# Compressed attention branch moved between the attention tiles, first token tile's heads finished ahead of the last tile

## The chip, the cores and the metric

The kernel runs on one core of one Trainium2 chip. The metric is device time in microseconds (us) for one execution. Five engines work side by side, each through its own queue in program order: TensorE (PE, matmuls and transposes), VectorE (DVE), ScalarE (ACT), GpSimd (POOL) and SyncE (SP, which issues the weight loads). They meet only through counting semaphores.

## The reference, cut to what matters

A decoder trunk of two layers, 256 tokens, model width 1024. Each layer is a mixer and a gated feed-forward network, each followed by a LayerNorm of `ALPHA*x + y`. The mixer's input projection feeds two halves. One is a short gated convolution of 512 channels. The other is attention of 8 query heads of 64 in 2 key/value groups with three branches:

```python
out = g0 * o_cmp + g1 * o_slc + g2 * o_win      # g = sigmoid(gates), per token and head
mixed = head_rmsnorm(concat([conv_out, attn_out]), head_norm_g)
x = layer_norm(ALPHA * x + mixed @ w_out)
```

`o_slc` and `o_win` are causal softmax attention over up to 256 keys. (At this length all blocks are selected and the window covers everything, so they differ only in their keys and values.) `o_cmp` is softmax attention over 15 compressed blocks of keys and values, which a small MLP makes out of 32 tokens each; a token sees only the blocks that have ended.

## The kernel before

**Tiles.** Tokens lie in two tiles `t` of 128. Projections are float32 products split in three (`mm3`: high by high, high by low, low by high). Weights come as 1 MB units through three `raw` buffers; ACT makes the high half of a unit (`split_hi`, L286), DVE the low half (`split_lo`, L290), into six ring slots.

**Attention units.** The two large branches are cut into 12 units `n` (`ATT`): branch, token tile, group, heads. Unit n goes through PE `scores` (banks 0 and 1 by parity) -> DVE `maxima` (L831, L833) -> ACT `exps` (L484) -> PE `transpose_p` (L1226, banks 6 and 7) -> DVE `copy_pT` (L841) -> PE `times_v` (L1239, into bank 2). `combine` on DVE (L849 to L863) weights what is summed in bank 2 and adds it to `acc`, once per branch and token tile (`og` 0 to 3, after units 1, 5, 7 and 11).

**Order.** The order on every engine is written out by hand. In PE's loop, step n issues `scores(n+2)`, `transpose_p(n+1)`, pieces of the convolution's projection, and `times_v(n)`. In DVE's loop, step n issues `maxima(n+1)`, `copy_pT(n)` and then what `between[n]` lists. In ACT's loop, step n issues `exps(n)` and then its own `between[n]`. Since queues are in order, what stands in `between[n]` of an engine is ahead of that engine's next unit.

**Compressed branch (thirteenth unit).** At PE's step 10, after `mean_squares(1)`, `cmp_scores` issues 24 matmuls of 30 columns into bank 0. After the loop DVE adds the mask, takes and subtracts the maximum (L1072 to L1078), ACT takes the exponential (L628), DVE sums, forms the factors and multiplies (L1082 to L1088). PE transposes (L1296), DVE copies, PE multiplies by the values (`times_v_cmp`, L1305, banks 7 and 2), DVE adds to `acc` (L881).

**Convolution and heads.** `mean_squares` (L1318), `copy_squares` (L895), POOL's `root` (L676, L678), `roots_high` and `roots_low`, `conv_roots` (L1328), `normalise_conv` (L906) and `mix_conv` / `mix_conv_low` (L498, L909) bring the convolution's heads to `xh`/`xl`. The attention heads of tile t go through ACT `square_heads` (L508), DVE `head_squares` (L886), POOL `root`, DVE `scale_heads` (L891), PE `heads_T` (L1348, bank 6+t), ACT `mix_high` and DVE `mix_low`. Both tiles' heads are done after the loop. Between these PE issues the output projection: `out_part(L, t, n, part)` is 6 matmuls of 512 columns on k-tile 2n+part, `out_unit` two of them. When tile 0's are all done (`y1_done`), DVE starts its LayerNorm while PE goes on with tile 1.

Of the kernel before, what the change touches and what calls it, by code (L numbers as in the profile page):

```python
# [59 lines left out]
N_ATT = 13  # L60
# [66 lines left out]
def build(nc, x, w_in, short_conv_w, cmp_pe, cmp_w1, cmp_b1, cmp_w2, cmp_b2, head_norm_g, w_out, ln1_g, ln1_b,  # L127
# [4 lines left out]
    with ExitStack() as ctx:  # L132
# [66 lines left out]
        smax = sb("smax", [P, N_ATT - 1, NPAIR])  # L199
# [24 lines left out]
        CMP_BANK = (7, 2)  # L224

# [25 lines left out]
        s_done, max_done, exp_done, cmp_p = sem("s_done"), sem("max_done"), sem("exp_done"), sem("cmp_p")  # L251
# [15 lines left out]


# [125 lines left out]
        def _(act):  # L394
# [109 lines left out]

            def square_heads(L, t):
# [48 lines left out]
            for L in range(DEPTH):  # L554
# [53 lines left out]
                for g in range(NG):  # L608
# [21 lines left out]
                mix_conv(L, 1)  # L630
                for t in range(TT):
                    square_heads(L, t)
                for t in range(TT):
                    act.wait_ge(mixT_done, 2 * L + t + 1)
                    for j in range(4):
                        mix_high(4 + j, xh[:, 4 + j, P * t:P * (t + 1)], bank[6 + t][:, P * j:P * (j + 1)])

                act.wait_ge(pv_done, 14 * L + 14)
# [27 lines left out]
        def _(pool):  # L666
# [57 lines left out]
        def _(dve):  # L724
# [110 lines left out]
            def copy_pT(L, n):  # L835
                dve.wait_ge(pT_done, N_ATT * L + n + 1)
                if n >= 2:
                    dve.wait_ge(pv_done, 14 * L + n - 1)
                width = 512 if n < 12 else 2 * P
                rows = P if n < 12 else NH * NBLK  # L840
                V.tensor_copy(probsT[n % 2][0:rows, 0:width], bank[6 + n % 2][0:rows, 0:width]).then_inc(pT_copied, 1)  # L841

            def combine(L, og, chain):
# [10 lines left out]
                dve.wait_ge(pv_done, 14 * L + O_READY[og])  # L854
# [5 lines left out]
                else:  # L860
                    V.tensor_tensor(part[:, 0, :].rearrange("p (h d) -> p h d", h=NH), o, c, ALU.mult).then_inc(o_read, 1)
                    dve.wait_ge(o_read, 4 * L + og + 1)
                    chain.mark(V.tensor_tensor(acc[:, t, :], acc[:, t, :], part[:, 0, :], ALU.add))  # L863
# [13 lines left out]
            def add_cmp(L, t, chain):  # L877

                dve.wait_ge(pv_done, 14 * L + 13 + t)
                chain.wait()  # L880
                V.tensor_tensor(acc[:, t, :], acc[:, t, :], bank[CMP_BANK[t]][:], ALU.add).then_inc(att_summed, 1)  # L881

# [28 lines left out]
            def mix_conv_low(L, pair):  # L911
                for j in (2 * pair, 2 * pair + 1):
                    dve.wait_ge(mix_hi, 12 * L + j + 1)
                    mix_low(j, xl[:, j, :], xh[:, j, :], conv_o[:, j, :])

# [68 lines left out]
            for L in range(DEPTH):  # L984
# [52 lines left out]
                for g in range(NG):  # L1037
# [13 lines left out]
                           3: [lambda: copy_squares(L, 0), lambda: split_lo(V, L, 15)], 4: [lambda: conv_gate(L, 1)],  # L1051
                           5: [lambda: split_lo(V, L, 16)],
                           6: [lambda: combine(L, 1, chain), lambda: split_lo(V, L, 17)],
                           7: [lambda: roots_low(L, 0), lambda: conv_taps(L, 1, chain)],
                           8: [lambda: combine(L, 2, chain), lambda: normalise_conv(L, 0)],
                           9: [lambda: conv_product(L, 1), lambda: mix_conv_low(L, 0)], 10: [lambda: split_lo(V, L, 18)]}
# [6 lines left out]
                copy_squares(L, 1)  # L1063
                split_lo(V, L, 19)
                copy_pT(L, 11)
                dve.wait_ge(s_done, N_ATT * L + 13)
                dve.wait_ge(pT_done, N_ATT * L + 11)
                flat = probs[0][:, 0:TT * NH * NBLK].rearrange("p (h c) -> p h c", c=NBLK)
                sc = probs[0][:, 0:TT * NH * NBLK].rearrange("p (t h c) -> p t h c", t=TT, h=NH)
                scores = bank[0][:, 0:TT * NH * NBLK].rearrange("p (t h c) -> p t h c", t=TT, h=NH)  # L1070
                for t in range(TT):
                    ins = V.tensor_tensor(sc[:, t], scores[:, t], bcast(cst[:, C_MA + NBLK * t:C_MA + NBLK * (t + 1)], 1,  # L1072
                                                                        [P, NH, NBLK]), ALU.add)
                chain.mark(ins)
                chain.wait()
                chain.mark(V.tensor_reduce(cmax[:], flat, AX.X, ALU.max))
                chain.wait()
                V.tensor_tensor(flat, flat, bcast(cmax[:], 2, [P, TT * NH, NBLK]), ALU.subtract).then_inc(max_done, 1)  # L1078
                roots_low(L, 1)
                dve.wait_ge(exp_done, N_ATT * L + 13)  # L1080
                for t in range(TT):
                    ins = V.tensor_reduce(rsum[:, 2, t].rearrange("p (g i) -> p i g", g=NG),  # L1082
                                          sc[:, t].rearrange("p (i g) c -> p i g c", g=NG), AX.X, ALU.add)
                chain.mark(ins)
                chain.wait()
                factors_cmp(L, chain)
                for t in range(TT):
                    ins = V.tensor_tensor(sc[:, t].rearrange("p (i g) c -> p i g c", g=NG),  # L1088
                                          sc[:, t].rearrange("p (i g) c -> p i g c", g=NG),
                                          coef[:, 2, t].rearrange("p (g i) -> p i g", g=NG).unsqueeze(3)  # L1090
                                          .to_broadcast([P, NPAIR, NG, NBLK]), ALU.mult)
                ins.then_inc(cmp_p, 1)
                combine(L, 3, chain)
                copy_pT(L, 12)
                normalise_conv(L, 1)
                for t in range(TT):
                    add_cmp(L, t, chain)
                head_squares(L, 0)
                mix_conv_low(L, 1)
                head_squares(L, 1)  # L1100
                for t in range(TT):
                    scale_heads(L, t)
                for t in range(TT):
                    dve.wait_ge(mix_hi, 12 * L + 8 + 4 * t)
                    for j in range(4):
                        tok = slice(P * t, P * (t + 1))
                        mix_low(4 + j, xl[:, 4 + j, tok], xh[:, 4 + j, tok], bank[6 + t][:, P * j:P * (j + 1)])
# [43 lines left out]
        def _(pe):  # L1151
# [128 lines left out]
            def cmp_scores(L):  # L1280

                pe.wait_ge(exp_done, N_ATT * L + 11)
                pe.wait_ge(cmp_copied, 2 * L + 1)
                for t in range(TT):
                    for h in range(NPAIR):
                        c0 = NG * NBLK * (NPAIR * t + h)
                        tok = slice(P * t, P * (t + 1))
                        ins = mm3(bank[0][:, c0:c0 + NG * NBLK], qTh[:, h, tok], qTl[:, h, tok],
                                  *(a[:].rearrange("p g c -> p (g c)") for a in (kcTh, kcTl)), True, True)
                ins.then_inc(s_done, 1)  # L1290

            def transpose_cmp(L):
                pe.wait_ge(cmp_p, L + 1)
                pe.wait_ge(pT_copied, N_ATT * L + 11)
                for t in range(TT):
                    ins = pe.transpose(bank[6][0:NH * NBLK, P * t:P * (t + 1)],  # L1296
                                       probs[0][:, NH * NBLK * t:NH * NBLK * (t + 1)], ident)
                ins.then_inc(pT_done, 1)

            def times_v_cmp(L, t):  # L1300
                pe.wait_ge(pT_copied, N_ATT * L + 13)
                pe.wait_ge(cmp_copied, 2 * L + 2)
                if t:
                    pe.wait_ge(o_read, 4 * L + 4)
                pe.matmul(bank[CMP_BANK[t]][:], probsT[0][0:NH * NBLK, P * t:P * (t + 1)], vbd.rearrange("p h d -> p (h d)"),  # L1305
                          start=True, stop=True).then_inc(pv_done, 1)
# [15 lines left out]
            def conv_roots(L, pair):  # L1322

                pe.wait_ge(roots_lo, 2 * L + pair + 1)
                for m in range(2):
# [6 lines left out]
            def out_product(L, t, c, k):  # L1332

                wh, wl = w_view(L, U_OUT + k // 2, 2)
# [323 lines left out]
```

## Time and profile before

| | |
|---|---|
| Median of 3 runs | 713.83 us (712.39 to 713.88) |
| Profiled execution, its own time | 709.42 us |
| Its span, first to last instruction | 707.6 us |
| PE busy | 98% of the span |
| DVE busy | 70% |
| ACT busy | 49% |
| Mean granted TensorE clock | 0.985 |

Busy time of PE overlaps from one matmul to the next, so a matmul's share of PE is read from the distance between starts, not from its own duration. A bracket behind a timeline row is the idle time of that engine just before it and what ended it. A granted clock of 1.00 is 2.4 GHz, 0.50 is 1.2 GHz.

### The profile page before, as it was taken

How to read it: one execution, taken by the hardware profiler on the slowest of the kernel's cores; microseconds unless marked ns; L12 is line 12 of the kernel's file. 1: busy time of each engine (PE TensorE's matmuls, PEld its weight loads, DVE VectorE, ACT ScalarE, POOL GpSimd, SP SyncE). 2: the span in 40 equal slices, each digit the busy share in tenths (PEclk: the TensorE clock that was granted, in tenths of full speed). 3: DMA queues.
4: the chain of work that ended last, by engine and by line, in shares of the span. 5: the costliest groups of instructions: out<-in, count | busy, mean ns of one | idle time of the engine just before them, and what ended most of it. 6: DMA issues, size and time to landing. Idle time of an engine off the chain costs nothing.

```text
span 707.6 us, 11957 instructions
## 1 busy us (share of the span) xinstructions
PE 690.6 (98%) x4822; PEld 631.8 (89%) x4822; DVE 492.1 (70%) x698; ACT 345.1 (49%) x492; POOL 158.6 (22%) x54
## 2 busy tenths in 40 slices
PE   8999999999999999999999999999999999999995
PEld 5899999888999999999778999988889999999994
DVE  4675768877996666666786457686869766666646
ACT  5654535414865444444347444453258555555520
POOL 0000020230174444440000000113106444444300
PEclk9999999899999999999999999997999999999998
DMA  9972443333875555556248143432357755555301
GB/s 290 323 249 62 142 156 119 120 119 106 282 241 195 191 195 196 194 188 179 78 148 269 61 150 118 152 102 78 119 200 245 269 179 179 179 178 178 119 0 60
DMA packets 87403, 116.85 MB, mean 165 GB/s; under 512 B 5230, under 2 KB 73536, under 8 KB 87360
## 3 DMA queue, kind: packets, MB, share of 16 engines
q1 hardware_dynamic: 85920, 111.85, 47.3%
q10 hardware_dynamic: 1440, 4.39, 1.8%
q8 instruction: 30, 0.49, 0.3%
q14 instruction: 13, 0.11, 0.0%
HBM read 115.19 MB, written 1.05 MB: 164 GB/s over the span
## 4 chain that ended last, share of the span: by engine, by line
PE 92%; DVE 5%; DMA 1%; issue 1%; ACT 1%; SPq 0%; DVEq 0%; ACTq 0%
PE bank L1154 28%; PE bank L1155 27%; PE bank L1156 27%; PE bank L1239 3%; PE bank L1226 2%; DMA x_tok<-in_x 1%; PE bank L1175 1%; DVE x_tok L941 1%; DVE stats L925 1%; DVE x_tok L923 1%; PE bank L1218 1%; DVE ring_lo L290 1%; DVE x_tok L949 1%; PE bank L1328 1%; PE bank L1305 0%
## 5 line engine op out<-in xcount | busy, mean ns | idle before, releaser
L290 DVE TENSOR_TENSOR ring_lo<-raw,ring_hi 128x2048 fp32r<-128x2048 f32 x102 | 232.5, 2284 | 21.6 <-ACT ring_hi L286 21.5
L1154 PE MATMUL bank<-xh,ring_hi 128*128 128x256 f32 x832 | 237.6, 286 | 0.0
L1156 PE MATMUL bank<-xh,ring_lo 128*128 128x256 f32 x832 | 235.8, 283 | 0.0
L1155 PE MATMUL bank<-xl,ring_hi 128*128 128x256 f32 x832 | 235.7, 283 | 0.0
L286 ACT ACTIVATE ring_hi<-raw 128x2048 fp32r<-128x2048 f32 x102 | 194.4, 1909 | 11.9 <-DMA raw<-in_w_in 9.1
L693 POOL COPY step_par<-ffn_par 128x16 f32 (+1 forms) x22 | 127.5, 5800 | 170.9 <-DVE work L962 170.9
L1154 PEld LDWEIGHTS bank<-xh,ring_hi 128*128 128x128 f32 x832 | 159.8, 192 | 0.9
L1155 PEld LDWEIGHTS bank<-xl,ring_hi 128*128 128x128 f32 x832 | 159.8, 192 | 0.6
L1156 PEld LDWEIGHTS bank<-xh,ring_lo 128*128 128x128 f32 x832 | 159.7, 192 | 0.0
L962 DVE SCALAR_TENSOR_TENSOR work<-bank,step_par,work 128x255 f32<-128x255 f32 (+1 forms) x176 | 72.2, 474 | 95.2 <-ACT work L532 95.1
L532 ACT ACTIVATE work<-bank,step_par 128x256 f32<-128x256 f32 x88 | 44.2, 560 | 117.1 <-PE bank L1156 117.1
L1154 PE MATMUL bank<-ring_hi,xh 128*128 128x512 f32 (+1 forms) x224 | 81.0, 362 | 3.8 <-DVE xl L754 3.8
L1154 PE MATMUL bank<-ring_hi,hTh 128*128 128x512 f32 (+1 forms) x224 | 80.8, 361 | 0.0
L1155 PE MATMUL bank<-ring_lo,hTh 128*128 128x512 f32 (+1 forms) x224 | 80.3, 359 | 0.0
L1156 PE MATMUL bank<-ring_hi,hTl 128*128 128x512 f32 (+1 forms) x224 | 80.1, 358 | 0.0
L1155 PE MATMUL bank<-ring_lo,xh 128*128 128x512 f32 (+1 forms) x224 | 77.9, 348 | 0.0
L1156 PE MATMUL bank<-ring_hi,xl 128*128 128x512 f32 (+1 forms) x224 | 77.9, 348 | 0.0
L676 POOL TENSOR_SCALAR cstat<-cstat 128x8 f32<-128x8 f32 x4 | 8.4, 2095 | 234.6 <-DVE cstat L895 234.6
L1154 PEld LDWEIGHTS bank<-ring_hi,xh 128*128 128x128 f32 x224 | 43.0, 192 | 10.8 <-DVE xl L754 3.8
L1156 PEld LDWEIGHTS bank<-ring_hi,xl 128*128 128x128 f32 x224 | 43.0, 192 | 5.3
L1155 PEld LDWEIGHTS bank<-ring_lo,xh 128*128 128x128 f32 x224 | 43.1, 192 | 5.0 <-issue 0.5
L484 ACT ACTIVATE probs<-bank,nmax 128x128 f32<-128x128 f32 (+1 forms) x64 | 26.1, 417 | 38.5 <-DVE nmax L833 38.5
(178 smaller groups left out, 785.6 us busy)
## 6 DMA issues: line engine op xcount, KB each, us to landing
raw<-in_w_up SPq DMA_DIRECT2D x44, 1024.0 KB, 5.2
raw<-in_w_down SPq DMA_DIRECT2D x22, 1024.0 KB, 5.3
raw<-in_w_in SPq DMA_DIRECT2D x21, 1024.0 KB, 5.2
raw<-in_cmp_w SPq DMA_DIRECT2D x8, 1024.0 KB, 5.9
raw<-in_w_out SPq DMA_DIRECT2D x8, 1024.0 KB, 4.9
qkv<-in_ln_g ACTq DMA_DIRECT2D x4, 512.0 KB, 3.4
qkv<-in_ln_b ACTq DMA_DIRECT2D x4, 512.0 KB, 4.9
raw<-in_w_in SPq DMA_DIRECT2D x2, 512.0 KB, 5.6
```

The costliest lines, as they stand in the source:

```text
L286: nc.scalar.activation(ring_hi[slot_of(L, u)][:], raw[raw_of(L, u)][:], ACT.Copy).then_inc(hi_done, 1)
L290: eng.tensor_tensor(ring_lo[slot_of(L, u)][:], raw[raw_of(L, u)][:], ring_hi[slot_of(L, u)][:].bitcast(fp32), ALU.subtract).then_inc(split ...
L484: ins = nc.scalar.activation(probs[n % 2][:, keys * j:keys * (j + 1)], bank[n % 2][:, keys * j:keys * (j + 1)], ACT.Exp, bias=nmax[:, n % ...
L532: ins = nc.scalar.activation(ffn_y[:, odd, v, c, :], bank[4 + 2 * odd + v][:, SEQ * c:SEQ * (c + 1)], ACT.Identity, scale=step_par[:, odd, ...
L676: chain.mark(nc.gpsimd.tensor_scalar(eps_out, var, mul, eps, ALU.mult, ALU.add))
L693: nc.gpsimd.tensor_copy(step_par[:, odd].rearrange("p v c k -> p (v c k)"), ffn_par[:, bass.ds(s, 1)].rearrange("p o v c k -> p (o v c k)"))\
L962: ins = V.scalar_tensor_tensor(ffn_y[:, odd, v, c, back:], b[:, SEQ * c:SEQ * (c + 1) - back], step_par[:, odd, v, c, 2 - back:3 - back], ...
L1154: pe.matmul(dst, ah, bh, start=start, stop=False, **kw)
L1155: pe.matmul(dst, ah, bl, start=False, stop=False, **kw)
L1156: return pe.matmul(dst, al, bh, start=False, stop=stop, **kw)
L1226: ins = pe.transpose(bank[6 + n % 2][:, P * m:P * (m + 1)], probs[n % 2][:, P * m:P * (m + 1)], ident)
L1239: ins = pe.matmul(bank[2][:, HEAD * (NPAIR * g + h):HEAD * (NPAIR * g + h + 1)], probsT[n % 2][:, P * (kb * j + b):P * (kb * j + b + 1)], ...
```

## The change

The compressed branch gets a place of its own: tiles `cmp_probs` and `cmp_pT`, bank 3, and semaphores of its own. Its parts move into the loops:

- PE: `cmp_scores` after `times_v(3)`, `transpose_cmp` after `times_v(5)`, `times_v_cmp(0)` and `(1)` after `times_v(6)` and `(7)`; `conv_roots(0)` now behind `times_v(8)` in step 8 instead of ahead of it.
- DVE: `cmp_maxima` in step 4, `cmp_weights` in 5, `copy_cmp_T` in 6, `add_cmp(0)` and `(1)` in 7 and 8.
- ACT: `cmp_exps` in step 5.

Tile 0's heads are finished inside the loops: `square_heads(0)` in ACT's step 8 behind `exps(8)`, DVE's `head_squares(0)` and `scale_heads(0)` in step 9 (with `normalise_conv(0)` moved there from 8 and `conv_product(1)` moved to 8), `heads_T(0)` in PE's step 11 and `mix_heads(0)` in ACT's step 11. POOL's order becomes conv 0, heads 0, conv 1, heads 1. The output projection behind the loop is reordered: for tile 0, k-tiles 2 and 3 come last, after the heads' k-tiles.

```diff
@@ ACT
-                           5: [lambda: conv_init(L, 1)], 6: [lambda: split_hi(act, L, 17)], 7: [lambda: roots_high(L, 0)],
-                           8: [lambda: split_hi(act, L, 18)], 9: [lambda: mix_conv(L, 0)], 10: [lambda: conv_square(L, 1)],
-                           11: [lambda: split_hi(act, L, 19)]}
+                           5: [lambda: cmp_exps(L), lambda: conv_init(L, 1)], 6: [lambda: split_hi(act, L, 17)],
+                           7: [lambda: roots_high(L, 0)],
+                           8: [lambda: square_heads(L, 0), lambda: split_hi(act, L, 18)], 9: [lambda: mix_conv(L, 0)],
+                           10: [lambda: conv_square(L, 1)], 11: [lambda: mix_heads(L, 0), lambda: split_hi(act, L, 19)]}
                 for n in range(2, 12):
                     exps(L, n)
                     for step in between.get(n, []):
                         step()
                 roots_high(L, 1)
-                act.wait_ge(max_done, N_ATT * L + 13)
-                flat = probs[0][:, 0:TT * NH * NBLK]
-                nc.scalar.activation(flat, flat, ACT.Exp, scale=SCALE).then_inc(exp_done, 1)
+                mix_conv(L, 1)
+                square_heads(L, 1)
                 split_hi(act, L, 20)
...
+                mix_heads(L, 1)
@@ POOL
-                for pair in range(2):
-                    conv_root_of(L, pair, chain)
                 for t in range(TT):
+                    conv_root_of(L, t, chain)
                     pool.wait_ge(att_ss, 2 * L + t + 1)
@@ DVE
+            def add_cmp(L, t):
+                dve.wait_ge(cmp_pv, 2 * L + t + 1)
+                dve.wait_ge(o_read, 4 * L + t + 1)
+                V.tensor_tensor(acc[:, t, :], acc[:, t, :], bank[3][:], ALU.add).then_inc(cmp_read, 1)
...
+                           4: [lambda: cmp_maxima(L, chain), lambda: conv_gate(L, 1)],
+                           5: [lambda: cmp_weights(L, chain), lambda: split_lo(V, L, 16)],
+                           6: [lambda: copy_cmp_T(L), lambda: combine(L, 1, chain), lambda: split_lo(V, L, 17)],
+                           7: [lambda: add_cmp(L, 0), lambda: roots_low(L, 0), lambda: conv_taps(L, 1, chain)],
+                           8: [lambda: add_cmp(L, 1), lambda: combine(L, 2, chain), lambda: conv_product(L, 1)],
+                           9: [lambda: normalise_conv(L, 0), lambda: head_squares(L, 0), lambda: mix_conv_low(L, 0),
+                               lambda: scale_heads(L, 0)],
+                           10: [lambda: split_lo(V, L, 18)]}
...
                 copy_squares(L, 1)
+                copy_pT(L, 11)
+                mix_heads_low(L, 0)
+                roots_low(L, 1)
+                combine(L, 3, chain)
+                normalise_conv(L, 1)
+                head_squares(L, 1)
+                mix_conv_low(L, 1)
+                scale_heads(L, 1)
                 split_lo(V, L, 19)
...
+                mix_heads_low(L, 1)
                 split_lo(V, L, 20)
@@ PE
                         mean_squares(L, 1)
-                        cmp_scores(L)
...
+                    if n == 10:
+                        out_part(L, 0, 0, 1)
+                    if n == 11:
+                        heads_T(L, 0)
+                    times_v(L, n)
+                    if n == 3:
+                        cmp_scores(L)
+                    if n == 5:
+                        transpose_cmp(L)
+                    if n in (6, 7):
+                        times_v_cmp(L, n - 6)
                     if n == 8:
                         conv_roots(L, 0)
-                    times_v(L, n)
-
-                out_part(L, 0, 0, 1)
-                transpose_cmp(L)
-                conv_roots(L, 1)
-                times_v_cmp(L, 0)
-                times_v_cmp(L, 1)
-                pe.wait_ge(exp_done, N_ATT * L + 13)
+
+                pe.wait_ge(exp_done, N_ATT * L + 12)
                 out_part(L, 1, 0, 0)
                 out_part(L, 1, 0, 1)
-                out_unit(L, 0, 1)
-                heads_T(L, 0)
+                conv_roots(L, 1)
+                out_unit(L, 0, 2)
+                out_part(L, 0, 3, 0)
+                heads_T(L, 1)
+                out_part(L, 0, 3, 1)
+                out_unit(L, 0, 1).then_inc(y1_done, 1)
                 for k in (2, 3):
                     out_product(L, 1, 0, k)
-                heads_T(L, 1)
-                out_unit(L, 0, 2)
-                out_unit(L, 0, 3).then_inc(y1_done, 1)
```

With the change, `combine(2)` and `combine(3)` are what signals `att_summed`, on which `square_heads(0)` and `(1)` wait.

## Rows read from the trace of the kernel before

**Rows 1.** The page: busy time of two engines, granted clock in 40 slices.

```profile
PE 690.6 (98%) x4822; PEld 631.8 (89%) x4822; DVE 492.1 (70%) x698; ACT 345.1 (49%) x492; POOL 158.6 (22%) x54
PEclk9999999899999999999999999997999999999998
```

**Rows 2.** Windows, PE alone: window, length, busy (count), granted clock, DMA.

```profile
112.00:130.30 18.30, 17.66 (x141) 1.00 0.22 67
130.30:137.10 6.80, 6.80 (x29) 0.50 0.93 304
...
475.10:485.20 10.10, 10.10 (x44) 0.50 0.65 208
```

**Rows 3.** Timeline of PE, layer 0: start, duration, line, shapes, count.

```profile
120.17 0.60 PE L1226 MATMUL bank<-cst,probs 128*128 128x128 f32 x4
...
124.25 0.66 PE L1226 MATMUL bank<-cst,probs 128*128 128x128 f32 x4 [0.64 <-ACT probs L484]
124.74 1.00 PE L1239 MATMUL bank<-qkv,probsT 128*128 128x64 f32 x8
...
127.03 0.95 PE L1318 MATMUL bank<-cst,conv_sq 128*128 128x2 f32 x8
127.84 0.26 PE L1154 MATMUL bank<-kcTh,qTh 128*128 128x30 f32 x1
...
130.07 0.26 PE L1156 MATMUL bank<-kcTh,qTl 128*128 128x30 f32 x1
...
138.46 1.93 PE L1305 MATMUL bank<-stage,probsT 120*128 120x512 f32 x4
139.82 0.80 PE L1154 MATMUL bank<-ring_hi,xh 128*128 128x512 f32 x1
...
145.46 0.39 PE L1156 MATMUL bank<-ring_hi,xl 128*128 128x512 f32 x1
```

**Rows 4.** Timeline of DVE, layer 0.

```profile
118.01 0.69 DVE L831 TENSOR_REDUCE smax<-bank 128x2 f32<-128x512 f32 x1
...
119.41 0.16 DVE L849 TENSOR_TENSOR coef<-rsum,egate 128x8 f32<-128x8 f32 x1
...
120.57 0.69 DVE L863 TENSOR_TENSOR work<-work 128x512 f32<-128x512 f32 x1
121.65 0.69 DVE L906 TENSOR_TENSOR conv_o<-conv_o,bank 128x512 f32<-128x512 f32 x1 [0.39 <-PE bank L1328]
...
132.51 0.46 DVE L1072 TENSOR_TENSOR probs<-bank,cst 128x120 f32<-128x120 f32 x2
...
134.37 0.46 DVE L1082 TENSOR_REDUCE rsum<-probs 128x8 f32<-128x120 f32 x2
...
140.42 0.69 DVE L881 TENSOR_TENSOR work<-work,bank 128x512 f32<-128x512 f32 x1 [0.17 <-PE bank L1305]
141.03 0.68 DVE L886 TENSOR_REDUCE mstat<-work 128x8 f32<-128x512 f32 x1
```

**Rows 5.** Timeline of ACT, layer 0.

```profile
116.14 1.91 ACT L286 ACTIVATE ring_hi<-raw 128x2048 fp32r<-128x2048 f32 x1
118.93 0.47 ACT L484 ACTIVATE probs<-bank,nmax 128x256 f32<-128x256 f32 x1 [0.88 <-DVE nmax L833]
...
119.75 0.20 ACT L484 ACTIVATION_READ_ACCUMULATOR probs<-bank,nmax 128x1 f32 x1
122.37 0.91 ACT L498 ACTIVATE xh<-conv_o,par 128x256 fp32r<-128x256 f32 x2 [2.42 <-DVE conv_o L906]
...
140.29 0.63 ACT L508 ACTIVATE work<-work 128x512 f32<-128x512 f32 x1
```

**Rows 6.** Timeline of POOL, layer 0.

```profile
129.00 2.16 POOL L676 TENSOR_SCALAR cstat<-cstat 128x8 f32<-128x8 f32 x1 [28.64 <-DVE cstat L895]
131.25 1.65 POOL L678 TENSOR_TENSOR croot<-cstat,neg_half 128x8 f32<-128x8 f32 x1
141.90 0.25 POOL L676 TENSOR_SCALAR mstat<-mstat 128x8 f32<-128x8 f32 x1 [9.00 <-DVE mstat L886]
```

More of the change, by code:

```diff
@@ L266, in build, with mix_turn @@
         dve_seq, pool_seq = sem("dve_seq"), sem("pool_seq")
+        def mix_turn(L, t, k):
+            return 12 * L + (k + 1 if k < 2 else k + 5 if k < 4 else 6 * t + k - 1)
         def xT_turn(L, t, b):
@@ L503, in mix_conv, with cmp_exps, mix_heads @@
                     mix_high(j, xh[:, j, :], conv_o[:, j, :])
+            def cmp_exps(L):
+                act.wait_ge(cmp_max, L + 1)
+                nc.scalar.activation(cmp_probs[:], cmp_probs[:], ACT.Exp, scale=SCALE).then_inc(cmp_exp, 1)
+            def mix_heads(L, t):
+                act.wait_ge(mixT_done, 2 * L + t + 1)
+                for j in range(4):
+                    mix_high(4 + j, xh[:, 4 + j, P * t:P * (t + 1)], bank[6 + t][:, P * j:P * (j + 1)])
             def square_heads(L, t):
@@ L625, in _ @@
                 roots_high(L, 1)
-                act.wait_ge(max_done, N_ATT * L + 13)
-                flat = probs[0][:, 0:TT * NH * NBLK]
-                nc.scalar.activation(flat, flat, ACT.Exp, scale=SCALE).then_inc(exp_done, 1)
+                mix_conv(L, 1)
+                square_heads(L, 1)
                 split_hi(act, L, 20)
[L630 to L638, printed above, removed]
+                mix_heads(L, 1)
+                act.wait_ge(pv_done, N_ATT * L + 12)
                 act.wait_ge(rope_done, 2 * L + 2)
@@ L837, in copy_pT @@
                 if n >= 2:
[L838 to L841, printed above, removed]
+                    dve.wait_ge(pv_done, N_ATT * L + n - 1)
+                V.tensor_copy(probsT[n % 2][:], bank[6 + n % 2][:]).then_inc(pT_copied, 1)
             def combine(L, og, chain):
@@ L862, in combine @@
                     dve.wait_ge(o_read, 4 * L + og + 1)
-                    chain.mark(V.tensor_tensor(acc[:, t, :], acc[:, t, :], part[:, 0, :], ALU.add))
+                    dve.wait_ge(cmp_read, 2 * L + t + 1)
+                    V.tensor_tensor(acc[:, t, :], acc[:, t, :], part[:, 0, :], ALU.add).then_inc(att_summed, 1)
             def factors_cmp(L, chain):
@@ new lines, in _, with cmp_maxima @@
+            c_all = cmp_probs[:].rearrange("p (h c) -> p h c", c=NBLK)
+            c_tok = cmp_probs[:].rearrange("p (t h c) -> p t h c", t=TT, h=NH)
+            def cmp_maxima(L, chain):
+                dve.wait_ge(cmp_s, L + 1)
+                scores = bank[3][:, 0:TT * NH * NBLK].rearrange("p (t h c) -> p t h c", t=TT, h=NH)
+                for t in range(TT):
+                    ins = V.tensor_tensor(c_tok[:, t], scores[:, t], bcast(cst[:, C_MA + NBLK * t:C_MA + NBLK * (t + 1)], 1,
+                                                                           [P, NH, NBLK]), ALU.add)
+                chain.mark(ins)
+                chain.wait()
+                chain.mark(V.tensor_reduce(cmax[:], c_all, AX.X, ALU.max))
+                chain.wait()
+                V.tensor_tensor(c_all, c_all, bcast(cmax[:], 2, [P, TT * NH, NBLK]), ALU.subtract).then_inc(cmp_max, 1)
@@ new lines, in cmp_weights @@
+            def cmp_weights(L, chain):
+                dve.wait_ge(cmp_exp, L + 1)
+                for t in range(TT):
+                    ins = V.tensor_reduce(rsum[:, 2, t].rearrange("p (g i) -> p i g", g=NG),
+                                          c_tok[:, t].rearrange("p (i g) c -> p i g c", g=NG), AX.X, ALU.add)
+                chain.mark(ins)
+                chain.wait()
+                factors_cmp(L, chain)
+                for t in range(TT):
+                    ins = V.tensor_tensor(c_tok[:, t].rearrange("p (i g) c -> p i g c", g=NG),
+                                          c_tok[:, t].rearrange("p (i g) c -> p i g c", g=NG),
+                                          coef[:, 2, t].rearrange("p (g i) -> p i g", g=NG).unsqueeze(3)
+                                          .to_broadcast([P, NPAIR, NG, NBLK]), ALU.mult)
+                ins.then_inc(cmp_p, 1)
@@ L883, in head_squares, with copy_cmp_T @@
+            def copy_cmp_T(L):
+                dve.wait_ge(cmp_T, L + 1)
+                V.tensor_copy(cmp_pT[:], bank[3][0:NH * NBLK, 0:TT * P]).then_inc(cmp_T_copied, 1)
             def head_squares(L, t):
@@ L912, in mix_conv_low, with mix_heads_low @@
                 for j in (2 * pair, 2 * pair + 1):
-                    dve.wait_ge(mix_hi, 12 * L + j + 1)
+                    dve.wait_ge(mix_hi, mix_turn(L, 0, j))
                     mix_low(j, xl[:, j, :], xh[:, j, :], conv_o[:, j, :])
+            def mix_heads_low(L, t):
+                tok = slice(P * t, P * (t + 1))
+                dve.wait_ge(mix_hi, mix_turn(L, t, 7))
+                for j in range(4):
+                    mix_low(4 + j, xl[:, 4 + j, tok], xh[:, 4 + j, tok], bank[6 + t][:, P * j:P * (j + 1)])
             def residual(L, which, t, n, banks, chain):
@@ L1050, in _ @@
                 between = {2: [lambda: combine(L, 0, chain), lambda: split_lo(V, L, 14)],
[L1051 to L1056, printed above, removed]
+                           3: [lambda: copy_squares(L, 0), lambda: split_lo(V, L, 15)],
+                           4: [lambda: cmp_maxima(L, chain), lambda: conv_gate(L, 1)],
[6 more added lines that the diff above has]
+                           10: [lambda: split_lo(V, L, 18)]}
                 for n in range(2, 11):
@@ L1071, in _ @@
[L1071 to L1107, printed above, removed]
+                copy_pT(L, 11)
```

55 lines of the change are left out of this document (25 added, 30 removed).

## The prediction

> **What bounds the kernel now.** I read the page first. PE is busy 98% of the span, and the granted clock is full except in two slices of the 40 that lie well inside the run [rows 1]. So a gain must come from PE: its waits, its work, or its clock. The change takes no matmul away and adds none. What is left to win is waits and clock.
>
> Next I cut the attention's end into windows. The clock is at 0.50 (1.2 GHz) for 6.8 us in layer 0 and 10.1 us in layer 1, and at 1.00 around them [rows 2]. Then I read PE's timeline for what PE did before it fell: a wait of 0.64 us and small transposes, six dense matmuls, then 8 matmuls of 2 columns and 24 of 30 columns, from 127.03 to the fall at about 130.3, 3.2 us with hardly a column in the array [rows 3]. The wait alone did not bring it down, nor did the same `mean_squares` of pair 0 earlier in the layer, around which dense work stands.
>
> Last I followed the two engines that feed PE. A unit's path is `maxima` -> `exps` -> transposes. ACT's own work is light, but it is an in-order queue, and what stands ahead of an `exps` delays that unit's transposes on PE. That is where this change puts new waits.
>
> **What can be won.** At 0.50 every matmul takes twice its time, so half of the slow stretches is lost: 3.4 + 5.1 = 8.5 us. The wait at 124.25 (0.64 in the row, about 0.8 from the mask matmul's issue to the transposes) falls once a layer: 1.6 us. Tile 0's LayerNorm is covered by 30 matmuls of tile 1 instead of 24; no row prices it, the bounds are 0 and one such wait, and I take 0.4 a layer, 0.8. Together 10.9 us.
>
> **What the change adds in work.** Nothing on PE. Its small matmuls start every 0.11 us ((130.07 - 127.84) / 20), so `cmp_scores` is 24 x 0.11 = 2.7 us; two transposes are 0.15; `times_v_cmp` is about 0.9 each (138.46 to 139.82 for two, with the long first matmul behind them) [rows 3]. These 4.6 us move from the end into steps 3 to 7. On DVE the mask and maxima are 1.4 us (132.51 on), the weights 1.7 (134.37 on), the copy 0.4, each `add_cmp` 0.7 [rows 4]; moved too. DVE is idle for over 5 us in steps 4 to 6 and can take them there. Both engines come later to step 8 by nearly the same 4.5 us, so differences between them can be read from the old times. No DMA is moved; the split of unit 18 is, by what now stands ahead of it.
>
> **Hold 1, step 8.** ACT now does `exps(8)`, `square_heads(0)`, `split_hi(18)`, `exps(9)`. `square_heads(0)` waits for `combine(2)`, which DVE issues after `maxima(9)`, `copy_pT(8)` and the new `add_cmp(1)`. In old times: `combine(2)` ends at 120.57 + 0.69 = 121.3, with `add_cmp` 121.9 [rows 4]; square 0.63 and split 1.91 give 124.5; `exps(9)` lasts from 118.93 to 119.95, 1.0, so it ends at 125.5 [rows 5]. PE was at `transpose_p(9)` at 120.17 [rows 3]. That is 5.3 us of standing; I take 5.2. Behind the waiting ACT instruction stand the split and `exps(9)`; behind the transposes stands all of PE.
>
> **Hold 2, step 9.** `mix_conv(0)` stands ahead of `exps(10)` as before, but `normalise_conv(0)` now comes after `copy_pT(9)`, and `conv_roots(0)` after `times_v(8)`. From the end of `exps(9)`: transposes 0.4, `times_v` 1.0 [rows 3], eight small matmuls and their end 1.1, normalise 0.69 [rows 4], `mix_conv` 0.91, `exps(10)` 1.0 [rows 5]: 5.1 us. PE has 0.4 + 1.0 + 0.9 and seven score matmuls (1.0) to do meanwhile, 3.3. Hold: 1.8.
>
> **Hold 3, step 10.** `scale_heads(0)` stands on DVE ahead of `maxima(11)` and waits for POOL. From the end of normalise: `head_squares` 0.68, start 0.2, POOL's first operation 2.16 after a long idle (0.25 after a short one; by then POOL has been idle for over 30 us), 0.1, 1.65 [rows 6], scale 0.7, maxima 0.9, `exps(11)` 1.0: 7.4. PE's way to the same transposes: `mix_conv` and `exps(10)` 1.9, then 3.6 us (124.25 to 127.84) [rows 3]: 5.5. Hold: 1.9 (nothing, were POOL's first operation 0.25).
>
> **Holds 4 and 5, behind the loop.** From `heads_T(0)`: four `mix_high` 1.2, `split_hi(19)` 1.9, `roots_high(1)` 0.65, `roots_low(1)` 0.7 make 4.45, against `times_v(11)` and 12 dense matmuls at 0.23 (139.82 to 145.46 holds 23 of them), 3.75: hold 0.7 at `conv_roots(1)`. From there: `combine(3)` 1.85 (119.41 to 121.26), normalise 0.69 [rows 4], mix 0.91, square 0.63 [rows 5], reduce 0.68, POOL 2.2 (its first operation short now), scale 0.7 make 7.65, against 0.9 + 18 x 0.23 = 5.0: hold 2.6 at `heads_T(1)`. In before both tiles' heads had 24 matmuls to hide behind; now 18 cover tile 1's.
>
> Holds per layer: 5.2 + 1.8 + 1.9 + 0.7 + 2.6 = 12.2; two layers 24.4. Less 10.9: **+13.5 us** at full clock.
>
> **The clock.** No row shows an idle PE of 5 us inside the run. The nearest is 3.2 us of nearly empty work, after which the clock fell [rows 3]; an idle array has done less. I take it that it falls in hold 1. Then transposes, `times_v(8)` and `conv_roots(0)`, all on hold 2's path, take 2.3 us more: 4.6 in two layers; what follows is partly hidden by hold 3. The bounds are 0 and half of a stretch like those seen, 5.1 a layer. Three other places a layer are near what brought it down: `cmp_scores` behind `times_v(3)` (1.0 us of 64 columns, then 2.7 of 30 columns, 3.7 us in a row against 3.2), hold 3 behind `mean_squares(1)`, and hold 5. Bounds there are 0 and 3.4 each (half of 6.8); dense work follows each, so I take 1.7, for half of six places, less what holds hide: 4. In all +8.6.
>
> The Trainium skill (TensorE: Matmul & The Clock Gate, "HAM oscillation — how this bites in real kernels") says that each long wait between bursts of matmuls throttles the clock again and that the cost is paid at every one. This trace agrees in that both layers fell once at the same place (6.8 and 10.1 us). It speaks against this change, which makes one such hole of many small ones; it is rival C below. [...]
>
> **Sum.** 24.4 - 10.9 + 8.6 = +22 us. Against the profiled execution: span 707.6 -> 729.7, own time 709.42 -> 731.5. Its own time lies 4.4 under the median of the runs, so I add to the median: 713.83 + 22 = **735.8 us**.
>
> **Rivals.**
> A. The holds are there but the clock stays up, in hold 1 too: +13.5, 727.3 us. For it: 0.64 us of idling did no harm. Against: eight times as long. 0.2.
> B. Faster: the holds are not on PE's way, because DVE with more work is behind in all of steps 4 to 8 and ACT's queue waits for it anyway; then the 10.9 us are won: 702.9. It decides where the holds of a layer sum to under 5.4 us. For it: PE issues dense convolution work up to step 7. Against: none is left in step 8, and hold 1 alone is 5.2 from three rows. 0.08.
> C. The clock falls at every hold and at `cmp_scores`, and for stretches like layer 1's: four places a layer at 1.7 to 5.1, say 3, is 24, less what holds hide (5): 13.5 + 19 = +32, 746. By the rule above this is what would come. Against it: dense work behind each. 0.12.
> D. Holds partly filled: hold 3 without POOL's long first operation and hold 1 at 4, and few falls: +3 to +10, 717 to 724. 0.1.
> The forecast: 0.5, itself 730 to 741.
>
> **Numbers.** The range must leave out no more than 0.2: B whole (0.08), the lower part of D and the upper of C (0.06 each) lie outside 722 to 746. A measurement tells 0.2% (1.4 us) from no change. Faster: nearly all of B, 0.07. Same: 0.02, between B and D. Slower: 0.91.
>
> **What would show it.** In the profile after: on PE the wait before L1226 of unit 9 with ACT as releaser, about 5 us; on ACT the `square_heads` row ahead of a `split_hi` and late `exps`; waits on `exps` of about 1.8 us twice more; L1348 waiting for DVE's `scale_heads`, 2 to 3 us; a granted clock of 0.50 right behind the first of them, and the old slow stretch behind `mean_squares` gone or shorter. POOL's L676 of about 2 us at tile 0's heads. Wrong would be: PE at `transpose_p(9)` without a wait (then hold 1 falls and B comes), or the holds there and the clock at 1.00 throughout (A).

## The result

The changed kernel takes 738.99 us (median of 4 runs, 733.62 to 739.11) against 713.11 us of the kernel before in the same session: a ratio of 1.0366, 95% interval 1.0318 to 1.0413. It is 25.9 us slower; 22 were forecast. The profiled execution has a span of 737.2 us, 29.6 above the one of before.

The page of the changed kernel, its busy row and its clock in 40 slices, answers to [rows 1]:

```profile
PE 703.8 (95%) x4822; PEld 643.1 (87%) x4822; DVE 492.6 (67%) x698; ACT 343.9 (47%) x492; POOL 154.2 (21%) x54
PEclk9999999589999999999999999876999999999998
```

The instruction counts are the same as before. What changed is when PE could run, and how fast. PE's waits in the changed kernel (total, times, longest):

```profile
PE bank L1245 <- ACT probs L490: 11.1, 4, 4.8
PE bank L1369 <- DVE work L935: 4.6, 2, 2.3
...
PE bank L1347 <- DVE hTl L944: 1.3, 2, 0.6
```

L1245 is `transpose_p`, L1369 `heads_T`, L1347 `conv_roots`. Together 17.0 us, against 1.3 in the kernel before, where only the 0.64 us wait of [rows 3] stood here, once a layer. The timeline of PE in layer 0 of the changed kernel shows where they stand:

```profile
125.80 0.28 PE L1237 MATMUL bank<-cmask_b,ident_b 128*128 128x256 bf16 x1
130.89 1.11 PE L1245 MATMUL bank<-cst,probs 128*128 128x128 f32 x4 [4.81 <-ACT probs L490]
...
137.94 1.11 PE L1245 MATMUL bank<-cst,probs 128*128 128x128 f32 x4 [0.72 <-ACT probs L490]
...
143.12 1.70 PE L1336 MATMUL bank<-cst,conv_sq 128*128 128x2 f32 x8
144.68 1.09 PE L1245 MATMUL bank<-cst,probs 128*128 128x128 f32 x4
...
153.75 0.33 PE L1347 MATMUL bank<-ident_r,hTh 128*128 128x128 f32 x1 [0.64 <-DVE hTl L944]
...
161.31 0.95 PE L1369 MATMUL bank<-cst,work 128*128 128x128 f32 x4 [2.29 <-DVE work L935]
```

The first is hold 1, the second hold 2, the last two holds 4 and 5. Hold 3 is missing: at 144.68 the transposes of unit 11 follow the mean squares without a wait. ACT's timeline shows why hold 1 is there (square L524, split L292, exponentials L490):

```profile
120.88 0.20 ACT L490 ACTIVATION_READ_ACCUMULATOR probs<-bank,nmax 128x1 f32 x1
127.50 0.63 ACT L524 ACTIVATE work<-work 128x512 f32<-128x512 f32 x1 [6.42 <-DVE work L871]
128.03 1.89 ACT L292 ACTIVATE ring_hi<-raw 128x2048 fp32r<-128x2048 f32 x1
129.84 0.45 ACT L490 ACTIVATE probs<-bank,nmax 128x256 f32<-128x256 f32 x1
```

`exps(9)` could have started at about 124.3 (DVE's L842 of that unit starts at 124.17); ACT sat 6.42 us at the square ahead of it.

Windows of PE in the changed kernel, layer 0 and then layer 1, laid on the stretches at half clock (compare [rows 2]):

```profile
106.90:110.30 3.40, 3.40 (x19) 0.50 0.00 0
...
130.90:147.80 16.90, 16.18 (x63) 0.50 0.19 62
161.70:165.00 3.30, 3.30 (x10) 0.51 0.45 161
...
465.40:472.00 6.60, 6.60 (x32) 0.50 0.00 0
...
492.90:509.10 16.20, 15.48 (x61) 0.50 0.17 53
523.40:526.60 3.20, 3.20 (x11) 0.50 0.41 137
```

Each layer has three: behind `cmp_scores`, from within hold 1 on (127.4 in layer 0), and at hold 5. Cut into windows of 1 us and summed as 2 x (1 - clock), they last 3.4 + 20.5 + 3.4 us in layer 0 and 6.8 + 20.5 + 3.4 in layer 1, 58.0 together. PE was idle for 8.5 of them, in the rest of hold 1 and in hold 2, 4.2 or 4.3 a layer. Before, the stretches at half clock came to 17.1 us, all of it with PE busy.

### The profile page after: what moved, and what is told of

It reads as the page before. It is cut to its first block, busy times and chain, and to the rows that moved or that the text cites. A ratio compares the mean times of both kernels' runs of the same rounds, so it can differ in the third digit from the quotient of the medians.

```text
span 737.2 us, 11955 instructions
## 1 busy us (share of the span) xinstructions
PE 703.8 (95%) x4822; PEld 643.1 (87%) x4822; DVE 492.6 (67%) x698; ACT 343.9 (47%) x492; POOL 154.2 (21%) x54
## 4 chain that ended last, share of the span: by engine, by line
PE 88%; DVE 5%; ACT 2%; issue 1%; DMA 1%; POOL 1%; SPq 0%; ACTq 0%; DVEq 0%; POOLq 0%
PE bank L1173 26%; PE bank L1174 26%; PE bank L1175 26%; PE bank L1258 3%; PE bank L1245 2%; DMA x_tok<-in_x 1%; ACT ring_hi L292 1%; PE bank L1194 1%; PE bank L1237 1%; DVE x_tok L991 1%; DVE stats L975 1%; PE bank L1336 1%; DVE ring_lo L296 1%; DVE x_tok L973 1%; ACT probs L490 1%
## 5 line engine op out<-in xcount | busy, mean ns | idle before, releaser
L292 ACT ACTIVATE ring_hi<-raw 128x2048 fp32r<-128x2048 f32 x102 | 194.4, 1909 | 12.4 <-DMA raw<-in_w_in 9.1
L548 ACT ACTIVATE work<-bank,step_par 128x256 f32<-128x256 f32 x88 | 44.4, 561 | 117.1 <-PE bank L1175 117.1
L1173 PE MATMUL bank<-ring_hi,xh 128*128 128x512 f32 (+1 forms) x224 | 82.5, 368 | 3.9 <-DVE xl L763 3.9
L1174 PE MATMUL bank<-ring_lo,xh 128*128 128x512 f32 (+1 forms) x224 | 79.9, 357 | 0.0
L1175 PE MATMUL bank<-ring_hi,xl 128*128 128x512 f32 (+1 forms) x224 | 79.6, 355 | 0.0
L1173 PEld LDWEIGHTS bank<-ring_hi,xh 128*128 128x128 f32 x224 | 44.4, 198 | 10.2 <-DVE xl L763 3.8
L1174 PEld LDWEIGHTS bank<-ring_lo,xh 128*128 128x128 f32 x224 | 44.4, 198 | 4.9
L490 ACT ACTIVATE probs<-bank,nmax 128x128 f32<-128x128 f32 (+1 forms) x64 | 26.1, 416 | 41.5 <-DVE nmax L842 41.5
L686 POOL TENSOR_SCALAR cstat<-cstat 128x8 f32<-128x8 f32 x4 | 4.4, 1112 | 189.4 <-DVE cstat L939 189.4
```

The source lines that it names most:

```text
L292: nc.scalar.activation(ring_hi[slot_of(L, u)][:], raw[raw_of(L, u)][:], ACT.Copy).then_inc(hi_done, 1)
L490: ins = nc.scalar.activation(probs[n % 2][:, keys * j:keys * (j + 1)], bank[n % 2][:, keys * j:keys * (j + 1)], ACT.Exp, bias=nmax[:, n % ...
L548: ins = nc.scalar.activation(ffn_y[:, odd, v, c, :], bank[4 + 2 * odd + v][:, SEQ * c:SEQ * (c + 1)], ACT.Identity, scale=step_par[:, odd, ...
L1173: pe.matmul(dst, ah, bh, start=start, stop=False, **kw)
L1174: pe.matmul(dst, ah, bl, start=False, stop=False, **kw)
L1175: return pe.matmul(dst, al, bh, start=False, stop=stop, **kw)
```

## The experiments

Every run below is described by two numbers beside its time: how long PE waits in the attention part, and how long it works at half clock. The table at the end of this section puts them together.

**Hold 1 taken away.** One step of ACT moved:

```diff
-  8: [square_heads(L, 0), split_hi(act, L, 18)], 9: [mix_conv(L, 0)],
+  8: [split_hi(act, L, 18)], 9: [square_heads(L, 0), mix_conv(L, 0)],
```

> The changed kernel with one step of ACT moved: square_heads(0) from step 8, ahead of split_hi(18) and exps(9), to step 9, behind exps(9) and ahead of mix_conv(0). Theory: hold 1 (4.8 us of waiting a layer in the profile after) is gone, and with it the long stretch at half clock of about 20 us that begins in it; holds 2 to 5 stay. That gives back 2 x 4.8 and some 5 us a layer of matmuls at half clock: about 719 to 725 us. Rival, that PE and DVE are both late in step 8 and ACT's order does not matter: 735 to 740, with the wait at transpose_p(9) now put down to DVE.

Measured: 721.75 us, ratio to the kernel before 1.0153 (1.0082 to 1.0223), span 718.7, 18.5 less than the changed kernel's profile. Its waits of PE:

```profile
PE bank L1369 <- DVE work L935: 4.6, 2, 2.3
PE bank L1245 <- ACT probs L490: 4.0, 2, 2.0
```

The wait at unit 9 is gone, and hold 2 shows at its full-clock size, 2.0 us instead of 0.72. The stretch of 20.5 us is now 6.8 in both layers. The first stretch of layer 1, which lies ahead of the edit, is also 3.4 us shorter here; that is worth about 1.7 of the 18.5. One misplaced activation cost over half of the loss.

**Hold 1 filled.** The holds stay; PE gets something to do:

```diff
+                    if n == 8:
+                        pe.wait_ge(z_done, 2 * L + 2)
+                        keep_busy(bank[4], 22)
                     if n < 11:
                         transpose_p(L, n + 1)
```

> The changed kernel with the holds left as they are, but 22 matmuls of 512 bf16 columns on idle data (about 4.7 us) issued on PE ahead of transpose_p(9), into bank 4, whose content is used up. They do no work for the output. Theory (idling brings the clock down, and the low clock costs as much again as the hold): the clock stays at 1.00 through steps 8 and 9, and the time falls by 8 to 14 us, to 725 to 731. Rival, that only the holds count and the half clock is hidden behind them: 737 to 740. A second rival, that the clock falls later all the same because of mean_squares and the other holds: 733 to 737.

Measured: 730.07 us, ratio 1.0272 (1.0200 to 1.0344), span 725.3. PE ran through the hold and beyond at full clock (windows of PE):

```profile
124.00:131.00 7.00, 6.89 (x33) 1.00 0.00 0
131.00:136.00 5.00, 3.49 (x29) 1.00 0.00 0
```

`transpose_p(9)` starts at 130.72 instead of 130.89, so the hold itself is untouched, and hold 2 is longer (1.5 us instead of 0.72). The 11.9 us less in span, 8.9 in the medians, therefore come from the clock; about 1.7 of them from the first stretch of layer 1, which is 3.4 us shorter here too and lies ahead of the edit. The second rival had a part too: in each layer a stretch of 3.4 us at half clock came later, behind hold 2.

**The branch alone.** The compressed branch as in the change, both tiles' heads and the output projection behind the loop as before (`square_heads(0)`, `head_squares(0)`, `scale_heads(0)`, `heads_T(0)`, `mix_heads(0)` taken out of the loops, POOL's and PE's last part in their old order):

> Half of the change: the compressed branch in bank 3 and in the loops as in the changed kernel, with the heads of both tiles finished behind the loop and the output projection in its old order. Theory (the loss comes from finishing tile 0's heads in ACT's and DVE's queues): holds 1, 3, 4 and 5 are gone, the slow stretch behind mean_squares(1) too; hold 2 (under 2 us) and the fall of the clock behind cmp_scores (1.7 to 3.4 us a layer) stay: 705 to 713. Rival, that the branch's own work on DVE in steps 4 to 8 is what makes PE late: 722 to 735.

Measured: 725.51 us, ratio 1.0196 (1.0128 to 1.0265), span 723.7. The expectation was missed by 12 us, though not for the rival's reason. Its waits of PE:

```profile
PE bank L1249 <- ACT probs L490: 4.0, 2, 2.0
...
PE bank L1262 <- DVE probsT L851: 2.2, 2, 1.7
```

Hold 2 is 2.0 us, and a new one of 1.7 us stands in layer 0, at `times_v(11)`: `copy_pT(11)` sits behind `split_lo(19)` on DVE. The kernel before has the same order on DVE, but there `cmp_scores` stood between the mean squares and the transposes of unit 11, and the split was over (131.1) before these transposes were; with `cmp_scores` moved away nothing covers it. The clock is at half for 37.5 us in sum; that was the larger part of the miss. So the branch brings no gain while its neighbours still wait.

**The small matmuls spread.** `cmp_scores` made a generator, one step of it behind each three matmuls of step 3's convolution pieces:

```diff
+                    extra = cmp_scores(L) if n == 3 else None
                     for _ in range(per_unit[n]):
-                        conv_unit(L, *pieces.pop(0))
+                        conv_unit(L, *pieces.pop(0), extra=extra)
...
-                    if n == 3:
-                        cmp_scores(L)
```

> The changed kernel with the 24 small matmuls of cmp_scores no longer in a row behind times_v(3), but in threes between the threes of 256 columns of step 3's convolution work. Theory (the row of small matmuls brings the clock down there): the first stretch at half clock (3.4 us in layer 0, 6.8 in layer 1) is gone, 2 to 5 us less: 733 to 737. Rival, that the clock falls there whatever the order, because of the small matmuls of the attention units around it: 738 to 740.

Measured: 732.72 us, just under the expected range, ratio 1.0307 (1.0237 to 1.0378), span 730.3. Windows of PE over the place in both layers:

```profile
97.00:112.00 15.00, 15.00 (x127) 1.00 0.28 99
458.00:474.00 16.00, 16.00 (x135) 1.00 0.27 93
```

The first stretch of either layer is gone. The holds are the same to 0.1 us. In layer 0 the long stretch was 13.7 us here instead of 20.5, though the edit does not touch what stands there; part of the gain is that.

**The branch alone, mended.** On top of the two edits above: `conv_roots(0)` into bank 4, which nobody uses in steps 5 to 9, and ahead of `times_v(8)` again; `normalise_conv(0)` back in step 8; `copy_pT(11)` ahead of `split_lo(19)`; `square_heads(0)` in ACT's step 11 and `head_squares(0)` right behind the loop. An excerpt of the edit, against the branch alone:

```diff
-  8: [add_cmp(L, 1), combine(L, 2, chain), conv_product(L, 1)], 9: [normalise_conv(L, 0), mix_conv_low(L, 0)],
+  8: [add_cmp(L, 1), combine(L, 2, chain), normalise_conv(L, 0)], 9: [conv_product(L, 1), mix_conv_low(L, 0)],
...
-                split_lo(V, L, 19)
                 copy_pT(L, 11)
+                head_squares(L, 0)
+                split_lo(V, L, 19)
```

> The branch alone, put together from what the runs so far showed: heads behind the loop, cmp_scores spread among step 3's convolution work, conv_roots(0) back ahead of times_v(8) and into bank 4, which is free there, normalise_conv(0) back in DVE's step 8, and behind the loop copy_pT(11) ahead of split_lo(19), tile 0's squares early. Theory (time is what PE waits plus half of what it works at half clock): no hold over 1 us in the loop and no stretch at half clock except perhaps one of 3.4 us a layer, so 698 to 705 us, 7 to 12 us under the kernel before. Rival, that the clock falls in the attention tiles as soon as the work there is thin, whatever the order: 708 to 718.

Measured: 704.6 us (11 runs, 703.07 to 709.27), against 710.84 of the kernel before beside it; ratio 0.9935, interval 0.9902 to 0.9967: 0.65% faster than the kernel before, a small gain, but the interval lies wholly under 1. Waits of PE, and then windows of PE over the attention part of both layers:

```profile
PE bank L1250 <- ACT probs L490: 1.3, 2, 0.6
```

```profile
90.00:160.00 70.00, 68.59 (x464) 1.00 0.37 121
436.00:506.00 70.00, 68.58 (x465) 1.00 0.37 121
```

The span is 701.5 us, and in this profiled execution (703.33 us, one of the fastest) the clock never falls in either. It does in others: the runs of 703.07 to 703.33 us have a mean granted clock of 0.996 to 0.998, the five of 706.01 to 709.27 us one of 0.986 to 0.991.

**The row of small matmuls in the mended version.** Only the spreading undone:

> The version with the branch alone in its mended order (heads behind the loop, bank 4 for conv_roots(0)), but cmp_scores in a row behind times_v(3) as in the change. Theory: the clock falls there again, 3.4 to 6.8 us a layer at 0.50, and half of that is lost: 4 to 7 us over the spread version, 708 to 712. Rival, that the fall there is hidden by DVE, which waits for PE in that step: within 1.5 us of the spread version.

Measured: 710.07 us (12 runs), span 706.1, ratio to the kernel before 0.9982 (0.9946 to 1.0017): 5.5 us over the spread version's median, 4.6 by the spans, with nearly the same holds (2.1 us in all instead of 2.4) and two stretches at half clock, 6.8 us in layer 0 and 3.4 in layer 1, each beginning at the row or just behind it (101.62 to 104.99 in layer 0, 448.04 to 450.87 in layer 1). Windows of PE:

```profile
102.00:103.00 1.00, 1.00 (x11) 1.00 0.45 172
103.00:104.00 1.00, 1.00 (x10) 0.86 0.00 0
104.00:105.00 1.00, 1.00 (x6) 0.50 0.00 0
...
451.00:452.00 1.00, 1.00 (x10) 0.94 0.00 0
452.00:453.00 1.00, 1.00 (x5) 0.50 0.00 0
```

The profiles of all kernels here say the same. In the six with the row behind `times_v(3)` the clock fell in both layers, from 1.3 us before the row's end to 2.2 us behind it, and stayed down for 3.4 or 6.8 us; in the three with it spread (scores spread, mended branch, heads ahead) it fell there in neither.

**The kernel before with its small matmuls spread.** In step 10, two threes of `cmp_scores` behind each three matmuls of `out_part(0,0)`, whose second half comes forward for that, and `out_part(1,0,0)` behind the loop in its place:

> The kernel before with its 24 small matmuls of step 10 spread among both parts of out_part(0,0), and out_part(1,0,0) in the place behind the loop that this leaves empty. Nothing else of the change. Theory: the two slow stretches (6.8 and 10.2 us) are gone, of which half was lost, 8.5 us; but with the clock up, PE waits at the transposes of the compressed branch for DVE's chain, which the slow clock had covered, 1 to 2 us a layer: 5 to 7 us less than before. Rival, that the clock falls because of the waits and the small transposes and not because of the row of small matmuls: no change.

Measured: 715.32 us, ratio 1.0085 (1.0052 to 1.0119): slower by 0.85%, and neither side foresaw it. Layer 0 stays at full clock. In layer 1 the clock falls twice, before and in the edited stretch. Windows of PE:

```profile
469.00:473.00 4.00, 3.78 (x17) 0.57 0.00 0
475.00:494.00 19.00, 19.00 (x71) 0.55 0.34 109
```

The first of the two falls begins at about 469.4, right behind the 0.64 us wait, in instructions that are the same as in the kernel before, where it did not fall there. So spreading the small matmuls does not by itself keep the clock up: here there were only the twelve dense matmuls of `out_part(0,0)` to spread 24 thin ones over, beside 8 of 2 columns. Whether that is why was not tested, and a reason for this one layer's falls was not found.

**Tile 0's heads ahead, without the holds in the loop.** The changed kernel with the spread scores, bank 4, `normalise_conv(0)` in step 8, `square_heads(0)` behind `mix_conv(0)` in ACT's step 9 and `scale_heads(0)` behind `copy_pT(10)`; the order behind the loop is the change's:

> The changed kernel with the holds inside the loop repaired and tile 0's heads still finished ahead of the last tile: cmp_scores spread in step 3, conv_roots(0) in bank 4 at its old place, normalise_conv(0) back in step 8, square_heads(0) behind mix_conv(0) in ACT's step 9, head_squares(0) at the end of DVE's step 9, scale_heads(0) in step 10 behind copy_pT(10). Only the order behind the loop is as in the changed kernel. Theory (holds 4 and 5 are a price of their own: 18 matmuls are too few to cover tile 1's heads): waits of 0.6 and 2.3 us a layer stay, perhaps one fall of the clock behind them, so 6 to 12 us over the version with the branch alone: 709 to 717. Rival, that finishing tile 0 early pays once nothing waits in the loop: 700 to 706.

Measured: 719.49 us (6 runs, 713.31 to 720.75), ratio 1.0109 (1.0038 to 1.0179), above the expectation; the profiled execution, its fastest, has a span of 711.5, 10 us over the mended branch alone; the medians are 14.9 apart. Its waits of PE:

```profile
PE bank L1375 <- DVE work L935: 4.5, 2, 2.3
PE bank L1246 <- ACT probs L490: 2.3, 2, 1.2
...
PE bank L1353 <- DVE hTl L944: 1.2, 2, 0.6
```

Holds 4 and 5 are unchanged: they belong to the order behind the loop, not to the loop. The runs spread over 7 us, and their mean granted clocks go with it: 0.987 at 713.31 us, 0.984 at 714.68, and 0.975 to 0.977 for the four of 719.35 to 720.75.

**POOL under a DVE operation.** `copy_squares(1)` moved ahead of `split_lo(18)`:

> The changed kernel with copy_squares(1) moved ahead of split_lo(18) on DVE, so that POOL's first operation on these squares starts while DVE is in its 2.28 us subtraction. If POOL's L686 is held by such a DVE operation, it lasts about 2 us instead of 0.20, as in the kernel before; if its length comes from how long POOL was idle, it stays at 0.2 to 0.33. DVE also waits for mean_squares(1) ahead of the split: the time is 736 to 741 either way.

Measured: POOL's L686 on these squares took 2.06 us; in the changed kernel it took 0.20. The three rows are POOL in the changed kernel:

```profile
136.83 0.33 POOL L686 TENSOR_SCALAR mstat<-mstat 128x8 f32<-128x8 f32 x1 [36.73 <-DVE mstat L930]
137.24 1.77 POOL L688 TENSOR_TENSOR mroot<-mstat,neg_half 128x8 f32<-128x8 f32 x1
145.22 0.20 POOL L686 TENSOR_SCALAR cstat<-cstat 128x8 f32<-128x8 f32 x1 [6.21 <-DVE cstat L939]
```

then POOL, and then DVE, in the experiment:

```profile
146.11 2.06 POOL L686 TENSOR_SCALAR cstat<-cstat 128x8 f32<-128x8 f32 x1 [5.76 <-DVE cstat L939]
```

```profile
145.83 2.28 DVE L296 TENSOR_TENSOR ring_lo<-raw,ring_hi 128x2048 fp32r<-128x2048 f32 x1
```

The POOL operation ends at 148.17, with the subtraction (148.11). Its single run took 734.92 us, 4 under the changed kernel and a little outside what was expected; the profile shows 44.4 us at half clock instead of 58.0.

**One table.** Waits: PE's waits in the attention part by the list of waits. Slow: time at half clock in which PE was busy. The sum is waits + slow / 2 (for the filled hold 9.4 more, its own matmuls). Measured is the span less 699.1 us, which is the mended branch's span less its waits.

| kernel | waits | slow | sum | measured |
|---|---|---|---|---|
| before | 1.3 | 17.1 | 9.9 | 8.5 |
| changed | 17.0 | 49.5 | 41.8 | 38.1 |
| hold 1 away | 10.5 | 23.8 | 22.4 | 19.6 |
| hold 1 filled | 8.8 + 9.4 | 20.5 | 28.5 | 26.2 |
| branch alone | 8.2 | 35.5 | 26.0 | 24.6 |
| scores spread | 17.0 | 34.8 | 34.4 | 31.2 |
| mended branch | 2.4 | 0 | 2.4 | 2.4 |
| mended, in a row | 2.1 | 10.2 | 7.2 | 7.0 |
| before, spread | 3.9 | 20.5 | 14.2 | 14.0 |
| heads ahead, mended | 8.0 | 13.7 | 14.8 | 12.4 |
| POOL under a DVE operation | 16.6 | 41.4 | 37.3 | 34.0 |

The mended branch agrees by construction; the other ten are explained to under 4 us by two columns. The sum is always a little high: where PE would have waited anyway, a slow matmul costs less than half of its time.

The same shows within one kernel. The kernel before ran 17 times in the session of the heads-ahead kernel and the mended one in a row, from 706.50 to 716.97 us, the same instructions each time, and its mean granted clock went from 0.993 to 0.973 with it. Fitted over these runs, each us more at half clock, taken as 2 x (1 - clock) x span, goes with 0.40 us more of span. A single profile is therefore one draw from such a spread, and differences of a few us between kernels are to be read from the medians.

## Why the prediction was right, point by point

- **Direction and size.** Right: 738.99 us against 735.8, inside 722 to 746. That it came so close is in part luck. By span, profile against profile, the change cost 29.6 us where the sum had 22; the sum was added to a median 4.4 us above the profiled execution. And two errors of opposite sign stand in it. The holds were put at 24.4 us and were 17.0, 7.4 too high. The clock was put at 8.6; what the span leaves beside the waits is 38.1 - 17.0 = 21.1, over 12 too low. Rival C's term for the clock, 19, was the nearer one.
- **Hold 1**, 5.2 us: measured 4.81 us idle, with `square_heads(0)` and `split_hi(18)` ahead of `exps(9)` as worked out. Moving the one step took it away.
- **Hold 2**, 1.8: 0.72 at half clock, where PE itself is late, and 2.0 and 1.5 at full clock in two experiments.
- **Holds 4 and 5**, 0.7 and 2.6: 0.64 and 2.29.
- **Hold 3**, 1.9: wrong; it did not appear. The step that failed was "POOL's first operation 2.16 after a long idle". In the changed kernel it took 0.33 us after 36.73 us of idling. The 2.16 of [rows 6] had another cause, which the moved copy showed: a DVE subtraction with both operands in SBUF, the on-chip memory, was running beside it. In the kernel before that was this one, which ends at 131.11, as POOL's operation ends at 131.16:

```profile
128.82 2.29 DVE L290 TENSOR_TENSOR ring_lo<-raw,ring_hi 128x2048 fp32r<-128x2048 f32 x1
```

  The Trainium skill (SBUF — State Buffer, "SBUF: two separate sides") says that a DVE operation with two SBUF inputs and a GpSimd operation that reads SBUF exclude each other for the length of an instruction; this trace agrees, 2.06 us against 0.20. With 0.33 in its place hold 3 shrinks to 0.1. The half clock took the rest: from the transposes of unit 10 (137.94) to those of unit 11 (144.68) PE needed 6.7 us where 3.6 were reckoned.
- **The clock**, +8.6 us: right in kind, too small. The stretch behind hold 1 was priced at 2.3 us a layer; it lasted 20.5, about 16 of them with PE busy, so some 8 a layer. The error was to let the clock come back with hold 2. The dense matmuls of `out_part(0,0,0)`, from 140.4 to the 143.12 of the row above, ran at half clock too, and it came back only at 147.9. Filling the hold gave back 11.9 us of span, about 10 without what lay ahead of the edit.
- **The other places**, half of six expected to fall: four of six did, at `cmp_scores` in both layers (3.4 and 6.8 us) and at hold 5 in both (3.4 each). Hold 3's place lay inside the long stretch.
- **What was to be won**, 10.9 us: the old slow stretches behind `mean_squares` went, as forecast, but only into others. The 0.8 taken for tile 0's LayerNorm does not show: the one wait of PE that follows layer 0's output projection, for DVE's low half of the normalised tokens, is 1.69 us in the kernel before, in the changed one and in the mended branch. A good half of the 10.9 can be had: the mended branch is 6.1 us of profiled span and 6.2 us of median under the kernel before.
- **Rival C**, the rule of the Trainium skill (TensorE: Matmul & The Clock Gate, "HAM oscillation — how this bites in real kernels") that a long wait between bursts of matmuls throttles the clock again each time. In the changed kernel it holds for the big hole of both layers (4.81 us) and for the small one at hold 5 (2.29), not for hold 4 (0.64). The two falls of the kernel before, which the prediction counts as agreeing with it, do not bear on it: no long wait stood ahead of them, PE was busy all through the small matmuls where they came [rows 3].

What stays open: why the clock fell in layer 1 and not in layer 0 of the spread kernel before, and why it falls in some executions of one kernel and not in others.

## What to carry to other kernels

When a step is put between others on an in-order queue, list what stands right behind it and who waits for that; here one 0.6 us activation ahead of a softmax tile cost 4.8 us a layer of matmul time, and then about as much again in clock. A queue full of thin matmuls can cost like a wait: in every profile with a row of 24 of 30 columns each behind `times_v(3)` the clock fell there, and the same 24 among the dense ones of the convolution did not bring it down. In the kernel before, spread over only twelve dense ones, they did not help. A part that is moved early gains nothing until the slow clock and the other waits it leaves behind are gone too, so look at both columns, waits and slow time, before and after each step.

## What the runs showed of the hardware

- Once down, the clock stayed at 1.2 GHz for 20.5 us in both layers of the changed kernel, although PE was busy for 16.2 of the last 16.9 us, with a dozen matmuls of 512 columns in it. Behind hold 5 of the same kernel it came back after 3.4 us.
- The same instructions can keep the clock in one kernel and lose it in another (469.4 in the spread kernel before), and in one execution and not in the next: 17 runs of the kernel before lie up to 10.5 us apart, with mean granted clocks of 0.993 to 0.973.
- A row of 24 matmuls of 30 columns, with PE busy throughout, was followed by a fall of the clock to 1.2 GHz in both layers of all six profiled kernels that had it behind `times_v(3)`, for 3.4 or 6.8 us; with the 24 spread among matmuls of 256 columns, in neither layer of three kernels.
- A small GpSimd operation takes 0.20 us alone and 2.06 us beside a 2.28 us VectorE subtraction of two SBUF operands.
